# A dense product stream of 3864 matmuls: moving operand and output taken from the last column to the first

## The reference, cut to what matters

```
first_block:  h = rms_norm(x); proj = h @ w_in          # 1024 -> 5408 columns
              y_a = rwkv7_time_mix(...); y_b = moba_attention(...)
              x = x + (g_a * (y_a @ w_branch_a) + g_b * (y_b @ w_branch_b)) @ w_out
              x = x + conv_ffn(rms_norm(x), w_up, conv, w_down)   # 2816 wide
second_block: for i in range(2):
                  m = fox_mixer(h, ...) if i == 0 else s5_mixer(h, ...)
                  x = x + rmsnorm(m)
                  x = x + rmsnorm((silu(h @ w_gate) * (h @ w_up)) @ w_down)
```

## Time and profile before

| | |
|---|---|
| median of three runs | 1163.75 us |
| span of the profiled execution | 1162.5 us (no separate time is given for this execution) |
| instructions | 18422 |
| TensorE matmul busy | 1114.6 us, 96% of the span, 7620 matmuls recorded |
| TensorE weight load busy | 917.4 us, 79% |
| VectorE busy | 783.4 us, 67% |
| ScalarE busy | 598.9 us, 52% |
| GpSimd busy | 119.7 us, 10% |
| chain that ended last | TensorE 80%, VectorE 12%, ScalarE 5% |
| mean granted TensorE clock | 0.988 of full speed |

### The profile page before, as it was taken

How to read it: one execution, slowest core, us unless ns; L and a number is a source line. 1 busy time by engine, 2 the same in 40 slices (tenths; PEclk the granted TensorE clock), 3 DMA queues, 4 the chain that set the end, 5 groups by cost and what they waited for, 6 DMA issues and landing times.

```text
span 1162.5 us, 18422 instructions
## 1 busy us (share of the span) xinstructions
PE 1114.6 (96%) x7620; PEld 917.4 (79%) x7620; DVE 783.4 (67%) x1268; ACT 598.9 (52%) x927; POOL 119.7 (10%) x122
## 2 busy tenths in 40 slices
PE   7999999999999999999998999999999799999997
PEld 6777878777888888888777887878878688888786
DVE  6747874658667775567566896887578868555543
ACT  6566523234565563466655664455572277345441
POOL 0405050500000000000000000012105400000000
PEclk9999999989999999999999999999999999999999
DMA  8533322014555555555323654555541245555551
GB/s 314 177 112 123 127 74 74 21 55 163 181 182 178 170 177 186 171 173 196 128 91 108 241 193 149 180 197 184 169 137 57 75 164 181 189 183 189 191 189 55
DMA packets 49668, 177.50 MB, mean 153 GB/s; under 512 B 5648, under 2 KB 6288, under 8 KB 49328
## 3 DMA queue, kind: packets, MB, share of 16 engines
q1 hardware_dynamic: 49440, 175.79, 44.8%
q10 hardware_dynamic: 144, 0.52, 0.1%
HBM read 175.25 MB, written 1.05 MB: 152 GB/s over the span
## 4 chain that ended last, share of the span: by engine, by line
PE 80%; DVE 12%; ACT 5%; issue 2%; POOL 1%; DMA 0%; SPq 0%; DVEq 0%; ACTq 0%
PE wps L2677 22%; PE wps L2678 21%; PE wps L2679 21%; PE tps L2666 5%; DVE wlo L1815 3%; ACT whi L1418 1%; PE wps L3121 1%; PE tps L2907 1%; DVE arena L2037 1%; PE tps L2912 1%; PE tps L2723 1%; DVE bt L2432 1%; PE tps L3087 1%; DVE bt L2443 1%; PE tps L2884 1%
## 5 line engine op out<-in xcount | busy, mean ns | idle before, releaser
L1815 DVE TENSOR_TENSOR wlo<-raw,whi 128x1024 fp32r<-128x1024 f32 (+1 forms) x322 | 390.3, 1231 | 178.5 <-ACT whi L1418 177.1
L2677 PE MATMUL wps<-whi,a_hi 128*128 128x512 f32 (+1 forms) x1008 | 401.5, 398 | 4.0 <-DVE wlo L1815 1.6
L2678 PE MATMUL wps<-whi,a_lo 128*128 128x512 f32 (+1 forms) x1008 | 392.3, 389 | 0.0
L2679 PE MATMUL wps<-wlo,a_hi 128*128 128x512 f32 (+1 forms) x1008 | 392.3, 389 | 0.0
L1418 ACT ACTIVATE whi<-raw 128x1024 fp32r<-128x1024 f32 (+1 forms) x322 | 327.4, 1052 | 79.3 <-PE wps L2679 79.0
L2677 PEld LDWEIGHTS wps<-whi,a_hi 128*128 128x128 f32 x1008 | 190.2, 189 | 45.1 <-issue 4.7
L2679 PEld LDWEIGHTS wps<-wlo,a_hi 128*128 128x128 f32 x1008 | 190.1, 189 | 39.9
L2678 PEld LDWEIGHTS wps<-whi,a_lo 128*128 128x128 f32 x1008 | 190.4, 189 | 36.4 <-issue 0.5
L2677 PE MATMUL wps<-whi,f_hi 128*128 128x512 f32 x264 | 104.8, 397 | 0.0
L2679 PE MATMUL wps<-wlo,f_hi 128*128 128x512 f32 x264 | 104.3, 395 | 0.0
L2678 PE MATMUL wps<-whi,f_lo 128*128 128x512 f32 x264 | 104.3, 395 | 0.0
(11 more groups left out here) (419 smaller groups left out, 1275.6 us busy)
## 6 DMA issues: line engine op xcount, KB each, us to landing
raw<-in_w_dn SPq DMA_DIRECT2D x22, 512.0 KB, 3.3
raw<-in_w_0dn SPq DMA_DIRECT2D x22, 512.0 KB, 3.3
raw<-in_w_1dn SPq DMA_DIRECT2D x22, 512.0 KB, 3.2
raw<-in_w_ua SPq DMA_DIRECT2D x20, 512.0 KB, 3.3
raw<-in_w_ub SPq DMA_DIRECT2D x20, 512.0 KB, 3.3
raw<-in_w_0ug SPq DMA_DIRECT2D x20, 512.0 KB, 3.4
raw<-in_w_0uu SPq DMA_DIRECT2D x20, 512.0 KB, 3.4
raw<-in_w_1ug SPq DMA_DIRECT2D x20, 512.0 KB, 3.3
```

The lines of the kernel that those rows point to most:

```text
L1815: V.tensor_tensor(t.wlo[n % NR][:, 0:w], t.raw[n % NR][:, 0:w], t.whi[n % NH][:, 0:w].bitcast(F32), ALU.subtract).then_inc(m.done(s.dve_lo ...
L2677: T.matmul(o, xh, wh, start=first, stop=False)
L2678: T.matmul(o, xl, wh, start=False, stop=False)
L2679: mm = T.matmul(o, xh, wl, start=False, stop=last)
```

## The change

In `product` the three matmuls take the moving operand through a view with step -1 along its columns, and write the output through a view with step -1. The stationary operands are as they were. Column c of the weights still ends in column c of the bank, and each sum has the same terms in the same order. Nothing else is touched: order of work, waits, signals, buffers, and evacuations.

```
-        T.matmul(o, xh, wh, start=first, stop=False)
-        T.matmul(o, xl, wh, start=False, stop=False)
-        mm = T.matmul(o, xh, wl, start=False, stop=last)
+        T.matmul(o[:, ::-1], xh, wh[:, ::-1], start=first, stop=False)
+        T.matmul(o[:, ::-1], xl, wh[:, ::-1], start=False, stop=False)
+        mm = T.matmul(o[:, ::-1], xh, wl[:, ::-1], start=False, stop=last)
```

## The result

The changed kernel took 1182.55 us (median of 4 runs, 1171.85 to 1185.95) against 1161.61 us of the kernel before in the same runs (median of 4): 1.0131 of it, 95% interval 1.0074 to 1.0189. A second comparison with 12 runs gave 1.0080 (1.0045 to 1.0115). The change makes the kernel slower by about 1%. The ratios in this document leave out executions that were disturbed: one of 2828.54 us of the kernel before, one of 1300.73 us in e12, and a few of the longest at the lowest clocks. No change was forecast, so the forecast was wrong; what came is rival B.

A forecast was written before the change was run, and what follows sets the result against it. TensorE, busy for 96% of the span and paced by its stream of columns, was taken as the bound. 1162.5 + 0 = 1162.5 us of span, forecast 1163.5 us as the runs' median lies 1.25 us higher; range 1156 to 1945 us.

The forecast's parts named there:

- rival B: Products with a_hi go to the slower pace of those with f_hi: +21 us at most, about 1178 us; chance 0.08.
- What bounds the kernel: TensorE, with a matmul in flight for 96% of the span, sets the pace through its stream of columns.
- The count: Dense products of 512 columns that the change reverses: 3024, and 792 with f_hi or f_lo as stationary operand.
- the two paces: Dense products at the same clock: 0.2267 us each with a_hi, 0.2336 us with f_hi.
- The write at nothing: Writing the sums to PSUM in descending order was taken to cost nothing.
- what I said of the last column: Which column is finished last is free, since a bank's readers wait for the group's last matmul.
- The read at nothing: Reading the moving operand in descending order was taken to cost nothing, after ScalarE's PSUM reads with a step.
- C: Products with f_hi go to the faster pace of 0.2267 us: -5.5 us, 1156 us in all; chance 0.07.
- Rival A: Every dense product: two columns no longer travel together, 0.43 us from start to start, 1931 us; chance 0.29.
- The test at 288 columns: Pace at 288 columns: 0.24 us would mean a cost per column, the same sum as at 512 one per matmul.
- D: The views are turned round again before the instruction is made, so nothing changes; time of the forecast, no chance of its own.

The follow-up runs named there:

- e12: Kernel before, ascending, with the f tiles moved by 192 bytes, run beside the changed kernel on one chip: 0.9932 of before, median 1159.29 us.
- e1: Kernel before with only the moving operand read from last column to first, sums written ascending: 1.0114 of before.
- e2: Kernel before with only the sums written from last column to first, moving operand read ascending: 0.9994 of before.
- e3: Kernel before, ascending, with 192 unused bytes ahead of the f tiles: 0.9939 of before.
- e4: Kernel before, ascending, with 320 unused bytes ahead of a_hi and a_lo: 1.0065 of before.
- e8: Kernel before with read and write in groups of 4 columns from last to first, ascending inside a group: 233.3 ns a product with a_hi and f.

## Why the prediction was wrong

*What bounds the kernel* was right in the main: four fifths of what was added to TensorE's busy time reached the end, 15.7 us of 19.6 in the pair e1 and e2. One sentence of it was too strong. The stationary load can't set the pace by its length, as the slabs of 288 columns show, but "So the stream of columns does" leaves out that the place of the stationary block counts: e3 and e4 moved that alone and changed the pace by 6.7 ns.

*The count* (3024 products with a and 792 with f) and *the two paces* were right, and so was their bound: +3024 x 0.0069 = 21 us at most. The a products gained 17.9 us, of which 13 to 14 remain at the end at equal clocks. Rival B's 1178 us stands against a median of 1182.55, and against 1178.45 in the longer comparison; that this one agrees so closely is in part luck, since B was priced with part of the products in mind, all of them changed pace, and the clock moves the medians by more than the difference.

*The write at nothing* was right, and so was what I said of the last column. That every matmul writes a column 512 columns after the one before holds only inside a call of `product`; between two calls for one bank lies a call for the other. This is the same in either direction and changes nothing.

*The read at nothing* is the step that failed: "I take nothing for the reading and nothing for the writing, since it is the nearest row in kind". The row was ScalarE's reading of PSUM with a step, which stands near the write. For the read from SBUF by an engine that reads two operands at once there was a much nearer pair, the a and f products: same shape, same clock, same signals, other addresses, 6.9 ns apart. I used it for the size of B and C and then set B at 0.08, "it would be chance that the reversed order brings it". What the runs showed in its place: the reversed read costs 6.7 ns in every settled a product, 226.7 to 233.3, with the write ascending as well (e1), and at each of eleven distances. With hindsight, and as an argument only: if the fast pace needs a certain relation between two address streams, a reversal is likely to break it in every matmul. Then B should have been the forecast for the a products, and C (a gain for f) unlikely, since the faster pace is the special one, as the table has it (two distances of nine).

*Rival A* was given 0.29 and is refuted: at a granted clock of 1.00 no stretch goes at 0.43 us. The argument against it, that neighbours stay neighbours, holds for the changed kernel, and in e8 as well. *The test at 288 columns* was to tell a cost per column from a cost per matmul; it is neither, for the loss there is under 1 ns. *Rival C* didn't come with the reversal; its price did, in e3, by an address. *D* is out: the pattern acted, by e1 against e2.

What isn't settled is the mechanism itself. That two reads meet inside SBUF or on the way into the array fits the runs but was shown by none directly, and it doesn't yet give the value at each distance. The reading order of the stationary operand wasn't tried.

## What to carry to other kernels

Where one shape of instruction has two paces at one clock, find out first what sets them: here it was worth 3% of a product's time, and 192 unused bytes brought 0.6% of the kernel. Where TensorE streams fp32r products of this shape (128 by 128 stationary, 512 columns moving) without pause, try stationary and moving tiles at a distance of a multiple of 256 bytes, and read the moving operand upward. Other shapes weren't tried, and at 288 columns no price was seen. A price for the read of an engine with two operand streams should be taken from rows of that engine at other addresses, not from another engine's rows.

## What the runs showed of the hardware that was not expected

The gaps fall on few values: 226.7, 233.3 and 240.0 ns, 6.7 ns apart, and mixtures of them. In the slow pace single gaps can alternate (231 and 236 ns in f1 before) while their mean stays at 233.3. After a pause the products with a_hi before have gaps between 224 and 240 ns, and only then settle at 226.7: after two gaps in 21 of 36 stretches, after four to ten in most of the others. So the fast pace is something that a stretch falls into; with f_hi before, or with a_hi reversed, none does.
